# Gate and up products of a ConvFFN by Strassen's seven block products, with memory laid out anew

## The reference, cut to what matters

```python
D_MODEL = 1024; SEQ = 1024; DEC_SEQ = 32; D_FF = 2816; CONV_F_WIDTH = 3

def conv_ffn(h, past_f, w_up, conv_w, w_down):
    z = h @ w_up                      # (frames, 1024) @ (1024, 2 * 2816)
    g, up = jnp.split(z, 2, axis=-1)
    gc, new_past_f = causal_dwconv(g, past_f, conv_w)     # 3 taps, depthwise
    return (jax.nn.silu(gc) * up) @ w_down, new_past_f

def trunk(x, ...):
    for l in range(DEPTH):            # DEPTH = 2
        h = rmsnorm(x, norm_mix[l])
        y = mixer_ab(h, ...) if l % 2 == 0 else mixer_c(h, ...)
        x = x + y
        h = rmsnorm(x, norm_ffn[l])
        y, pf = conv_ffn(h, past_f[l], w_up[l], conv_f_w[l], w_down[l])
        x = x + y
    return rmsnorm(x, norm_final), ...
```

## Time and profile before

| | us |
|---|---|
| median of 3 runs (lowest, highest) | 2303.43 (2303.33, 2305.65) |
| the profiled execution | 2298.37 |
| its span, first to last instruction | 2296.4 |
| PE busy | 2233.2 (97%) |
| DVE busy | 1316.3 (57%) |
| POOL busy | 612.5 (27%) |
| ACT busy | 474.4 (21%) |

### The profile page before, as it was taken

The page is one execution under the profiler, slowest core; times in us unless marked ns, Lnnn a source line. Parts: engine busy times, 40 slices in busy tenths (PEclk is TensorE's granted clock), DMA queues, the critical chain, the costliest instruction groups (busy, mean ns, idle before and its releaser), DMA issues.

```text
span 2296.4 us, 31368 instructions
## 1 busy us (share of the span) xinstructions
PE 2233.2 (97%) x14014; PEld 2216.2 (97%) x14014; DVE 1316.3 (57%) x1520; ACT 474.4 (21%) x518; POOL 612.5 (27%) x273
## 2 busy tenths in 40 slices
PE   7997999999999999999999999999999999999997
PEld 6987999999999999999999999999999999999996
DVE  6999855545565455555643524565554554555656
ACT  4443242111111111111301111232111111111113
POOL 4654332222222222222412222232222222222224
PEclk9998999999999999999999999999999999999998
DMA  4111311111111111111111111111111111111112
GB/s 152 38 37 32 110 40 47 47 47 46 47 47 47 47 47 46 47 47 47 38 46 47 47 47 47 47 40 47 45 45 46 47 47 47 47 47 47 46 49 76
DMA packets 33831, 115.06 MB, mean 50 GB/s; under 512 B 3808, under 2 KB 7136, under 8 KB 33696
## 3 DMA queue, kind: packets, MB, share of 16 engines
q1 hardware_dynamic: 33696, 113.06, 15.7%
HBM read 108.42 MB, written 4.62 MB: 49 GB/s over the span
## 4 chain that ended last, share of the span: by engine, by line
PE 80%; DVE 5%; issue 5%; POOL 0%; ACT 0%; DVEq 0%; POOLq 0%; ACTq 0%
PE psum L365 27%; PE psum L367 26%; PE psum L366 26%; DVE x L1040 1%; DVE psum L1121 1%; DVE x L1041 1%; DVE work L997 0%; DVE conv_s L1123 0%; DVE work L1016 0%; PE psum L427 0%; PE psum L438 0%; DVE act_lo L1218 0%; PE psum L517 0%; DVE sumsq L1020 0%; PE psum L608 0%
## 5 line engine op out<-in xcount | busy, mean ns | idle before, releaser
L365 PE MATMUL psum<-xg_hi,w_hi 128*128 128x352 f32 x3072 | 995.3, 324 | 24.8 <-DVE xg_lo L1025 16.3
L367 PE MATMUL psum<-xg_hi,w_lo 128*128 128x352 f32 x3072 | 989.8, 322 | 0.0
L366 PE MATMUL psum<-xg_lo,w_hi 128*128 128x352 f32 x3072 | 987.9, 322 | 0.0
L649 POOL TENSOR_TENSOR w_lo<-raw,w_hi 128x1024 fp32r<-128x1024 f32 x188 | 458.8, 2440 | 1541.3 <-ACT w_hi L763 1541.3
L365 PEld LDWEIGHTS psum<-xg_hi,w_hi 128*128 128x128 f32 x3072 | 578.1, 188 | 27.7 <-issue 10.0
L367 PEld LDWEIGHTS psum<-xg_hi,w_lo 128*128 128x128 f32 x3072 | 580.4, 189 | 0.0
L366 PEld LDWEIGHTS psum<-xg_lo,w_hi 128*128 128x128 f32 x3072 | 579.5, 189 | 0.0
L365 PE MATMUL psum<-act_hi,w_hi 128*128 128x352 f32 x1440 | 468.8, 326 | 10.3 <-DVE x L1041 7.6
L367 PE MATMUL psum<-act_hi,w_lo 128*128 128x352 f32 x1440 | 462.5, 321 | 0.0
L366 PE MATMUL psum<-act_lo,w_hi 128*128 128x352 f32 x1440 | 461.9, 321 | 0.0
L763 ACT ACTIVATE w_hi<-raw 128x1024 fp32r<-128x1024 f32 x188 | 198.9, 1058 | 1073.3 <-PE psum L367 1071.0
(11 more groups left out here) (137 smaller groups left out, 1161.0 us busy)
## 6 DMA issues: line engine op xcount, KB each, us to landing
raw<-slabs SPq DMA_DIRECT2D x188, 512.0 KB, 3.6
x<-x_t SPq DMA_DIRECT2D x16, 528.0 KB, 6.3
y_t<-x SPq DMA_DIRECT2D x6, 528.0 KB, 3.4
y_t<-x SPq DMA_DIRECT2D x3, 352.0 KB, 2.3
x<-mix SPq DMA_DIRECT2D x1, 512.0 KB, 3.3
const<-consts SPq DMA_DIRECT2D x1, 262.0 KB, 11.6
x<-bs SPq DMA_DIRECT2D x1, 256.0 KB, 3.6
x<-lnv SPq DMA_DIRECT2D x1, 128.0 KB, 3.8
```

What stands on the lines that cost most here:

```text
L365: nc.tensor.matmul(out, w_hi[:, s], hi, start=start, stop=False)
L366: nc.tensor.matmul(out, w_hi[:, s], lo, start=False, stop=False)
L367: return nc.tensor.matmul(out, w_lo[:, s], hi, start=False, stop=stop)
L649: nc.gpsimd.tensor_tensor(w_lo[:, s], raw[:, s], w_hi[:, s].bitcast(F32), ALU.subtract).then_inc(weights_ready, 1)
```

## The change

In both ConvFFN phases an up tile and the gate tile of the same hidden channels form a pair. The pair's product is cut in 2 x 2 blocks: over even and odd input tiles (4 each), over up and gate, and over the two halves of the columns (528 each, each as 2 parts of 264, one part a bank). Of the 8 block products Strassen's scheme (in Winograd's form) keeps 7. Each is a `group` of 2 parts x 4 tiles x 3 products, 24 matmuls of 264 columns. Groups 2, 4 and 6 go on top of group 0 in bank pair X (0 and 1, or 6 and 7), group 5 on top of group 3 in bank pair Z (4 and 5), group 1 is in Y (2 and 3). Before a bank is added to, ScalarE copies what it holds to SBUF (`part_copied`), and VectorE adds these copies: C11 = Y + copy, C22 = X + copy, C21 = Z + copy; C12 is what X holds in the end.

The sums of weight blocks (`sums`, four operations of 512 columns a pair) are made by VectorE in the raw slabs. w_hi and w_lo become rings of 4 entries of 512 columns; a group takes one entry, another slab two. There are 4 raw slots in place of 2.

The sums of input blocks T1 to T4 are made once a phase, in `combine`, which replaces `last_down` ahead of phases 1 and 3: for each pair of x tiles GpSimd makes the difference T1 (before the gain) and the low parts of T3 and T4, and adds all squares into one sum (`tile_sum`, 7 a phase); ScalarE rounds and squares; VectorE makes T2, T3, T4 and the low parts of the input, T1 and T2.

The order around it: the downward unit of a block now has the end of the gate before it (`gate_second_half`, taps) and the next pair's weight sums between its adds. The last downward unit of mixer C has 8 jobs of 36 matmuls in place of 16 of 18, the first two interleaved. Buffers of phase 0 are overlaid on the larger input buffers; single buffers replace some double ones. Indices that could be registers become constants.

```diff
             def split_product(...)   # now takes the weight columns; `reopen` adds to a closed bank
+            def group(slab, which, first_bank, opens, ready=None):
+                for h in range(2):
+                    for kp in range(KP):
+                        if ready is not None and h == 0:
+                            pe.wait_ge(ready[0], ready[1] + 2 * kp)
+                        at = kp * KP_COLS + which + h * PART
+                        last = split_product(psum[:, first_bank + h, 0:PART], tile_at(slab, kp),
+                                             xs_hi[:, at:at + PART], xs_lo[:, at:at + PART],
+                                             opens and kp == 0, kp == KP - 1, reopen=not opens)
+                return last
+            def pair(p, b, q):                                    # TensorE
...
+                group(weights(0), X_B11, x_bank, True, ...).then_inc(tile_done, 1)
...
+                group(weights(1), X_B21, Y_BANK, True, ...).then_inc(tile_done, 1)
+                pe.wait_ge(part_copied, 3 * n + 1)
+                group(weights(2), X_T2, x_bank, False, ...).then_inc(tile_done, 1)
...
+                group(weights(3), X_T3, Z_BANK, True, ...).then_inc(tile_done, 1)
+                if fresh:
+                    pe.wait_ge(tile_squares, (KD - 1) * (s + 1))
+                    rms_stats(p, psum[:, 7, 0:ROW_TILES])
+                pe.wait_ge(part_copied, 3 * n + 2)
+                group(weights(4), X_T1, x_bank, False, ...).then_inc(tile_done, 1)
+                pe.wait_ge(part_copied, 3 * n + 3)
+                group(weights(5), X_T4, Z_BANK, False, ...).then_inc(tile_done, 1)
+                if fresh:
+                    rms_spread(p, psum[:, Y_BANK, 300:300 + ROW_REST])
+                pe.wait_ge(tile_evacuated, pair_read(p, b, q, C22_READ))
+                group(weights(6), X_B22, x_bank, False).then_inc(tile_done, 1)
+            def down(p, b):                                       # TensorE
+                for m in range(KD):
...
+                    if m >= 2:
+                        pe.wait_ge(tile_evacuated, down_read(p, b, m - 2))
...
+            def combine(s, p, n0, read):                          # GpSimd
+                for kp in range(KP):
+                    diff(kp)
+                    if kp < 3:
+                        lo(p_before, n0 + 1 + kp)
+                    if kp:
+                        tile_sum(s, 2 * kp)
+                    if kp == 3:
+                        entry_lo(p, 0, 0, 2)
+                    t_lo(kp, 0)
+                    if kp == 3:
+                        entry_lo(p, 0, 0, 3)
...
+                    t_lo(kp, 1)
+                    if kp == 2:
+                        entry_lo(p, 0, 0, 0, 1)
+                    tile_sum(s, 2 * kp + 1)
+            def pair(p, at):                                      # ScalarE
...
+                nc.scalar.activation(two(half(prod[q], 1)), halves_of(x_bank), ACT.Copy).then_inc(part_copied, 1)
+                entry_hi(p, b, q, 4)
...
+                entry_hi(p, b, q, 5)
+                act.wait_ge(tile_done, group_done(p, b, q, 2))
+                nc.scalar.activation(two(half(prod[q], 0)), halves_of(x_bank), ACT.Copy).then_inc(part_copied, 1)
+                entry_hi(p, b, q, 6)
+                act.wait_ge(tile_done, group_done(p, b, q, 3))
+                act.wait_ge(tile_evacuated, pair_read(p, b, q, C11_READ))
+                nc.scalar.activation(two(half(prod[q], 1)), halves_of(Z_BANK), ACT.Copy).then_inc(part_copied, 1)
...
+                    entry_hi(p, after[1], after[2], 0, 1, 2)
+            def combine(s, p, add, read):                         # VectorE
+                for kp in range(KP):
+                    add(e)
+                    dve.scalar_tensor_tensor(xs(xs_lo, kp, X_B11), half(x_e, 0), g_e, ..., ALU.mult, ALU.subtract)
...
+                    add(o)
+                    dve.scalar_tensor_tensor(t2, half(x_o, 1), g_o, t1, ALU.mult, ALU.subtract)
+                    dve.scalar_tensor_tensor(t3, half(x_e, 0), g_e, t2, ALU.mult, ALU.subtract)
+                    dve.scalar_tensor_tensor(xs(xs_lo, kp, X_B21, COLS), x_o, g_o, ..., ALU.mult, ALU.subtract)
+                    low(xs(xs_lo, kp, X_T2), t2, xs(xs_hi, kp, X_T2)).then_inc(t12_ready, 1)
+                    dve.scalar_tensor_tensor(t4, half(x_o, 0), g_o, t2, ALU.mult, ALU.subtract)
+                    low(xs(xs_lo, kp, X_T1), t1, xs(xs_hi, kp, X_T1)).then_inc(t12_ready, 1)
+            def down(p, at):                                      # VectorE
+                gate_second_half(p, pb, pq)
+                conv_tap_k(p, pb, pq, 1)
+                ff_add(p, b, 0)
+                conv_tap_k(p, pb, pq, 2)
+                ff_add(p, b, 1)
+                if leads:
+                    sums(p, after[1], after[2], 1, step_of(p, before, 4))
+                ff_add(p, b, 2)
+                product(p, pb, pq)
+                ff_add(p, b, 3)
...
```

More of the change, by code:

```diff
@@ L105, in _jobs_after_slab, with slab_of, _tables @@
+def slab_of(p, unit, i=0):
+    return _unit_at(p, SLAB0, 2, 2, unit) + i
+def _tables():
+    released, last_step = [], []
     after = []
@@ L579, in _ @@
[L579 to L590 removed]
+                up_job(0, JOB_S[c] + 1, 12 + c, 1)
@@ new lines, in ffn @@
+            def ffn(p):
+                for unit in UNITS:
+                    if unit == ("pair", 0, 0):
+                        entry_lo(p, 0, 0, 4, 5, 6)
+                        r_of_frames(p)
+                    elif unit[0] == "pair":
+                        entry_lo(p, unit[1], unit[2], *range(GROUPS))
+                    else:
+                        for i in range(2):
+                            split_lo(step_of(p, unit, i), ring(p, unit, i), raw_at(slab_of(p, unit, i)))
+            lo(0, 0)
```

1364 lines of the change are left out of this document (899 added, 465 removed).

## The result

The changed kernel takes 2245.4 us (median of four, 2243.98 to 2246.42) where the kernel before takes 2303.56 (2303.33 to 2305.65): a ratio of 0.9735 (95% interval 0.9722 to 0.9748), 2.65% faster. The prediction was 2262, so the gain was 16.6 us larger than forecast. The profiled execution took 2244.46 us, its span is 2242.7.

What follows compares the result with a forecast made beforehand. TensorE bounds the kernel: time is the number of matmuls times their cadence. From 2298.4 us, blocks and pairs give -85.2 and transitions +44, so 2257.2, and with the median's 5.1 on top 2262 us; range 2230 to 2292.

Steps and rivals of the forecast that it cites:

- Cadence at 264 columns: Matmuls of gate/up pairs: 122.2 ns each with 12.2 ns per instruction; a pair goes from 22.88 to 20.53 us.
- The bound by weight loads: TensorE in pairs: one weight load per matmul permits 107 ns each, below the 122.2 ns taken.
- The rival that loads show through at 264 columns: Pairs: 188 ns loads show under streams 122 ns apart; at 135 ns the time is 2356 us; chance 0.11.
- The downward unit: Third downward tile of a block: TensorE waits 1.5 us for add 0, where it was 0.59; range 0 to 2.5.
- No wait inside pairs: Gate/up pairs: no stall counted; the C22 read before group 6 has 1.9 us of slack.
- The rival of the late C22 read: Pairs: VectorE's fixed order makes the C22 read 5 us late, +74 us in 24 pairs, 2336 us; chance 0.08.
- The transitions: Two transitions into feed-forward phases: TensorE loses 21 and 23 us, +44 together, at the statistics' wait for the last sum of squares.
- The serial sum: Each transition: GpSimd's 44.6 us and VectorE's SBUF work exclude each other, 67 us of one resource, ending near 392.8.
- Free transitions: Rival, both transitions: GpSimd's sums fall where VectorE reads PSUM, all ready by 374, time 2218 us; chance 0.22.
- double transitions: Rival, both transitions: they take twice the predicted sum, time 2306 us; chance 0.07.
- Parts at nothing: Overlaid memory and tables, raw weight slots, final stage and the mixer phase's 8 downward tiles: claimed to cost nothing.
- The offset: Whole kernel: the median of the runs is 5.1 us above the profiled execution, added to 2257.2 us.

Runs made afterwards that it cites:

- short streams: Changed kernel with the second and third product of each triple in pairs cut from 264 to 176 and 128 columns, same loads: 2226.88 us, 0.965 of the kernel before.

## Why the prediction was right, and where its sizes were off

- *Cadence at 264 columns.* 122.2 ns predicted, 122.1 measured. The 12.2 ns are per instruction, the value chosen. The bound by weight loads was closer than the prediction had it: its 107 ns were misread from the earlier trace rows, where a load of the common size takes 112, and the short streams fit 112 too. The rival that loads show through at 264 columns didn't come; its 135 ns were worked out from no row. With the mean of 189 columns of the run with short streams they seem to. By the gap rule of the Trainium skill ("TensorE: Matmul & The Clock Gate", Back-to-back issue gap) it would have been 112.5: the measurement disagrees, with 122.1. The section gives that rule for an isolated matmul; for a stream of weight loads and matmuls it gives some 81 ns at 128 columns and 131 at 512, and that isn't this kernel either, with 112 at 128 and 158.9 at 352.
- *The downward unit.* The wait of 1.5 came at the place, in the number (20) and by the mechanism named, but is 0.82 long, and worth 0.87 by its removal. The sum had the long subtraction and the second tap in series, 2.4 and 1.3; in the trace they end 4.1 after the subtraction's start (731.93 to 736.02), 0.4 more, yet add 0 starts at 735.95, and other terms of the sum were smaller. A block is 65.02 for 65.44. Over 20 blocks that is 8.4 us, and the mean block before was 69.32 in place of the 69.23 used, 1.8 more: together 10.2, where the phases gave 9.3 more than the 85.2 predicted.
- *No wait inside pairs.* Right in all blocks. The rival of the late C22 read is out.
- *The transitions.* 21 and 23 predicted, 21.5 and 19.45 measured at the landmarks: the size was right in the first and 3.5 too large in the second. With the 1.6 us that the first landmark had before its transition, both lose about the same, some 20; the two more that the interleaved tiles were to cost didn't come. The mechanism was right in what it names as the resource (GpSimd busy 55.71 of 84 us, 66%, against the 60% asked for) and wrong in what ends the time. Two of its signs were missed narrowly: TensorE's idle time was to be 15 to 25 us in each and is 14.5 and 15.6, and GpSimd's 1056-column sums were to last longer than 2.5 us and last 2.46 on average, 2.05 to 2.93. GpSimd's last sum of squares ended at 391.83, a microsecond from the predicted 392.8:

```profile
389.39 2.44 POOL L1013 TENSOR_TENSOR r_rows<-r_rows,work 128x1056 f32<-128x1056 f32 x1
```

  but TensorE was in group 3 until 396.2, so nothing waited for the sum. The loss came in five pieces (two low parts by GpSimd, an add and a low part by VectorE, ScalarE's copy), and 5.3 of the 22.3 us came from the half clock, which the prediction did not have as a term. That both roads lead to nearly the same number is in part luck. The serial sum is also no full model of these stretches: GpSimd stands idle for 28 of the 84 us while it waits for the adds and for ScalarE, and when its 17 us of sums were cut, the transitions got 9.7 and 7.4 shorter, not 17. The copy of bank X did cost its one or two (1.93).
- *Free transitions* (2218) and *double transitions* (2306): the first is out by 41 us of loss, the second by the same number. No run made the transitions free; with the sums cut they still cost some 18.
- *Parts at nothing* (phase 0, the memory layout, the mixer stage, the end): 0.0 and -0.1 by the table. The first stage has 1.6 us ahead of the transition, no more than it differs by between kernels with the same start.
- *The offset.* I carried the 5.1 us between the profiled execution and the median of before over to the changed kernel. There it is 0.9. The error of 16.6 is thus 9.3 (blocks), 3.0 (transitions) and 4.2 (offset), within 0.1.
- *The range.* The parts named for 2230 to 2292 (-22 for the cadence, -19 and +21 for the transitions, -30 and +20 for the downward unit) would add up to 2191 and 2303; how the narrower range comes from them isn't said. The result is in both. It lies 17 us below the forecast and 27 above the rival of free transitions, so it is the traces that decide between the two, and not the time.

## What to carry to other kernels

Trading TensorE products for additions pays by the cadence of the shorter instruction, not by the count of operations: here three quarters of the columns in 7/6 of the instructions (7/8 of the work) gave 89.7% of the time per pair, and the short streams got little out of fewer columns. What the additions cost is decided where they crowd: add up the SBUF work of VectorE and GpSimd as one resource, per stretch, and look for the place where it is above the stretch's length; inside the blocks it was hidden, in the two transitions and at one tile it was not. Cure such a place by taking work out of it, or by putting what TensorE waits for (here an add that reads PSUM, which GpSimd did not lengthen) ahead of what is lengthened. A change of order among the operations of the crowded stretch moved its waits and took none away in sum, before work was taken out and after it. And before a difference of a few us is put down to an edit, cut the stage into the part where the edit acts and the rest: here a stage was 3.4 us shorter while the transition in it, the only place that the edit changed, was 0.4 longer.

## What the runs showed of the hardware that was not expected

- Idle pieces of TensorE of 2 to 4 us cost more than their length. The clock was 0.92 over the 84 us of the first transition (some 13.5 us at 1.2 GHz; as 3.3 of them were idle anyway, the matmuls took 5.3 us longer, on top of 14.5 idle), and 0.50 from 382 to 386, between waits of 3.71 and 3.34 us and one of 1.93. The kernel before, without these waits, had 1.00 there. After 2.1 us of one-column matmuls the clock fell to half in some traces and not in others, on the same code: 1.6 us for the stretch behind.
- The same 352-column matmuls of mixer C, at full clock and without a wait, start 160.0 ns apart in seven programs with the new layout and 161.2 in the other three: 2.3 us over the stage. The one program that was traced twice has 161.2 both times.
- A wait of VectorE for GpSimd, or the other way, shows as a longer operation and not as idle time: the tap shows 3.33 us beside a 2.97 us subtraction and 1.32 alone, and ends 1.1 us after the subtraction (736.02 and 734.90); the subtraction is longer itself than the one 5.9 us earlier (2.97 against 2.40), and it started 0.05 us after a VectorE operation of 0.77 us. The add that reads PSUM took 0.88 or 0.89 either way.
- With streams of mixed length only an average can be read as a cadence. Starts 81 ns apart stand beside one of 175, while the weight loads start 108 to 128 ns apart; over a triple it comes to 115 a piece.
